# The FFNs' down products by Strassen's scheme: seven block products in place of eight per stretch of FFN units

## The reference

```python
def conv_ffn(xn, w_up, conv_w, conv_b, w_down):
    u = xn @ w_up                                  # 512 x 1024 by 1024 x 5632
    up = jnp.pad(u, ((0, 0), (CONV_WIDTH - 1, 0), (0, 0)))
    c = conv_b
    for j in range(CONV_WIDTH):                    # 3 taps along the tokens
        c = c + conv_w[j] * up[:, j:j + s]
    val, gate = jnp.split(c, 2, axis=-1)
    return (jax.nn.silu(gate) * val) @ w_down      # 512 x 2816 by 2816 x 1024

for layer in range(2):
    h = h + merge_heads(heads) @ w_out[layer]
    h = h + conv_ffn(rmsnorm(h, norm_ffn[layer]), w_up[layer], conv_w[layer], conv_b[layer], w_down[layer])
return rmsnorm(h, norm_final)
```

## Time and profile before

| what | value |
|---|---|
| median of 3 runs | 1738.47 us (1738.30 to 1738.47) |
| span of the profiled execution | 1736.7 us |
| its time by the runs, with what lies around the span | 1738.3 to 1738.47 us, some 1.7 us over the span |
| PE busy | 1724.0 us, 99% of the span |
| POOL busy | 1019.3 us, 59% |
| DVE busy | 947.7 us, 55% |
| ACT busy | 540.9 us, 31% |
| PE's share of the chain that ended last | 96% |

### The profile page before, as it was taken

The page is one execution under the profiler, slowest core; times in us unless marked ns, Lnnn a source line. Parts: engine busy times, 40 slices in busy tenths (PEclk is TensorE's granted clock), DMA queues, the critical chain, the costliest instruction groups (busy, mean ns, idle before and its releaser), DMA issues.

```text
span 1736.7 us, 24721 instructions
## 1 busy us (share of the span) xinstructions
PE 1724.0 (99%) x9676; PEld 1403.0 (81%) x9680; DVE 947.7 (55%) x1893; ACT 540.9 (31%) x1212; POOL 1019.3 (59%) x1046
## 2 busy tenths in 40 slices
PE   9999999999999999999999999999999999999998
PEld 7886787787689877789888888897777988888887
DVE  6997734785643355525661266237775366405643
ACT  4626532213423344432110011036663321101112
POOL 8524556562366744338776677656443587667763
PEclk9999999999999999999999999999999999999999
DMA  6322223221233311114323332323112233243321
GB/s 187 107 80 66 99 77 106 67 92 43 73 122 109 98 49 59 63 49 115 98 92 91 102 96 89 114 73 98 50 55 68 73 109 97 85 117 91 99 93 50
DMA packets 174196, 152.17 MB, mean 88 GB/s; under 512 B 5448, under 2 KB 149192, under 8 KB 174080
## 3 DMA queue, kind: packets, MB, share of 16 engines
q1 hardware_dynamic: 171904, 148.05, 28.1%
q10 hardware_dynamic: 2176, 2.53, 0.4%
HBM read 147.38 MB, written 2.14 MB: 86 GB/s over the span
## 4 chain that ended last, share of the span: by engine, by line
PE 96%; DVE 2%; ACT 1%; issue 0%; DVEq 0%; ACTq 0%
PE ps L302 80%; PE ps L2236 2%; PE ps L2256 2%; PE ps L2271 2%; PE ps L1703 1%; PE ps L373 1%; PE ps L1681 1%; PE ps L2244 1%; PE ps L1618 1%; PE ps L806 1%; PE ps L1639 1%; PE ps L1693 0%; PE ps L1627 0%; PE ps L813 0%; PE ps L756 0%; PE ps L781 0%
## 5 line engine op out<-in xcount | busy, mean ns | idle before, releaser
L146 POOL TENSOR_SCALAR w_hi<-w_raw 128x512 fp32r<-128x512 f32 x512 | 312.2, 637 | 671.9 <-PE ps L302 671.9
L150 POOL TENSOR_TENSOR w_lo<-w_raw,w_hi 128x512 fp32r<-128x512 f32 x512 | 687.2, 1373 | 11.1
L302 PE MATMUL ps<-x_hi,w_hi 128*128 128x512 f32 (+2 forms) x1432 | 532.3, 372 | 0.5 <-DVE x_lo L574 0.4
L302 PE MATMUL ps<-x_hi,w_lo 128*128 128x512 f32 (+2 forms) x1432 | 522.5, 365 | 0.0
L302 PE MATMUL ps<-x_lo,w_hi 128*128 128x512 f32 (+2 forms) x1432 | 522.0, 365 | 0.0
L302 PEld LDWEIGHTS ps<-x_hi,w_hi 128*128 128x128 f32 (+1 forms) x1432 | 269.3, 188 | 60.1 <-issue 16.5
L302 PEld LDWEIGHTS ps<-x_hi,w_lo 128*128 128x128 f32 (+1 forms) x1432 | 269.3, 188 | 44.3
L302 PEld LDWEIGHTS ps<-x_lo,w_hi 128*128 128x128 f32 (+1 forms) x1432 | 269.6, 188 | 40.1
L2553 DVE SCALAR_TENSOR_TENSOR ffn_cv<-ps,col,ffn_cv 128x510 f32<-128x510 f32 (+1 forms) x176 | 131.8, 749 | 192.7 <-ACT ffn_cv L2531 188.1
L2531 ACT ACTIVATE ffn_cv<-ps,col 128x512 f32<-128x512 f32 x88 | 63.8, 776 | 496.6 <-PE ps L302 496.6
L330 DVE TENSOR_TENSOR h<-h,ps 128x512 f32<-128x512 f32 x64 | 43.8, 687 | 258.9 <-PE ps L302 258.9
(11 more groups left out here) (372 smaller groups left out, 2426.5 us busy)
## 6 DMA issues: line engine op xcount, KB each, us to landing
w_raw<-w_up SPq DMA_DIRECT2D x88, 512.0 KB, 5.1
w_raw<-w_down SPq DMA_DIRECT2D x16, 1024.0 KB, 5.0
w_raw<-od_w_in SPq DMA_DIRECT2D x12, 1024.0 KB, 5.2
w_raw<-w_in_fox SPq DMA_DIRECT2D x10, 1024.0 KB, 5.3
w_raw<-w_in_dil SPq DMA_DIRECT2D x10, 1024.0 KB, 5.4
w_raw<-w_out SPq DMA_DIRECT2D x8, 1024.0 KB, 5.0
w_raw<-ev_w_in SPq DMA_DIRECT2D x6, 1024.0 KB, 5.7
w_raw<-w_down SPq DMA_DIRECT2D x8, 768.0 KB, 4.4
```

The source lines that it names most:

```text
L146: ins = pool.tensor_scalar(hi[:, c:min(c + PIECE, size)], raw[:, c:min(c + PIECE, size)], 1.0, 1.0, ALU.mult, ALU.mult)
L150: ins = pool.tensor_tensor(lo[:, c:min(c + PIECE, size)], raw[:, c:min(c + PIECE, size)], hi[:, c:min(c + PIECE, size)].bitcast(F32), ALU. ...
L302: mm = pe.matmul(o, l, r, start=start and i == 0, stop=stop and i == 2)
```

## The change

The down product of a stretch is taken as a 2 x 2 block product: the tokens in two halves of 256, the units in even and odd ones, the output columns in two halves of 512. In place of eight block products it makes seven (Strassen's scheme in Winograd's form), from sums and differences of the blocks.

- The stretches are 8, 8 and 6 units (`PARTS`), so four, four and three k tiles (`kk`) per block product. A block product is 2 token tiles x kk x 3 matmuls of 512 columns, and its weights are one slot. Per stretch the order is 1, 5, 2, 6, 7, 3, 4; products 5 and 2 first leave out the last k tile ("most") and make it up later ("last").
- Weights: POOL splits the slots of products 1, 5 and 2 as before, and makes four combinations of kk pieces of 512 (TENSOR_TENSOR). The `hi` of the slots 6, 7, 3 and 4 is made by ACT, the `lo` by DVE. A third raw buffer of four pieces holds quarter 22; the combinations lie in `w_chain`.
- Activations: a pair of units gives seven operand blocks of 256 tokens. DVE makes four sums of 256 (s1 to s4), ACT the `hi` (one of 256 and three of 512), DVE the `lo` (one of 256 and three of 512). DVE no longer works a unit ahead: conv(u), gate(u), first low, conv(u + 1), gate(u + 1), sums, lows.
- Sums: DVE adds or subtracts PSUM banks into `h` 16 times per stretch (`take`), in order with the weights' lows (`early`). TensorE accumulates on over several products in the same banks, so products 6, 7 and 3 wait for such reads.
- In the seam and the final stage each `last_tile` is now the half of product 3 or 4 for one token tile, 9 matmuls. `Final` takes for each tile the column half that is ready early first.
- The causal mask's place in SBUF serves as a part of the third raw buffer and the mask is loaded again after the first FFN; the tables of the second mixer are loaded after it too. Several semaphores are shared. Elsewhere only the counting of slots changes (`W.nth`).

The core of the diff:

```diff
+class Group:
+    ORDER = ("1", "5", "2", "6", "7", "3", "4")
+    LATE = ("6", "7", "3", "4")
+    def gpsimd(self, pool):
+        W, kk = self.W, self.kk
+        pool.wait_ge(W.loaded[self.a], self.arrived["11"])
+        W.halve(pool, self.slot("1"), W.raw[:, self.a, 0:kk * 512])
+        pool.wait_ge(W.loaded[self.b], self.arrived["12"])
+        if self.lows:
+            pool.wait_ge(W.lo_by_dve, self.lows)
+        for k in range(kk):
+            pool.tensor_tensor(self.chain(k), self.quarter(self.b, k), self.quarter(self.a, k), ALU.subtract).then_inc(W.combined, 1)
+        pool.wait_ge(W.combined, self.sums + kk)
+        W.halve(pool, self.slot("5"), W.chain[:, 0:kk * 512])
+        pool.wait_ge(W.loaded[self.a], self.arrived["21"])
+        W.halve(pool, self.slot("2"), W.raw[:, self.a, 0:kk * 512])
+        pool.wait_ge(W.loaded[RAW], self.arrived["22"])
+        pool.wait_ge(W.split_done, W.nth(self.slot("5")))
+        for k in range(kk):
+            pool.tensor_tensor(self.chain(k), self.quarter(RAW, k), self.chain(k), ALU.subtract).then_inc(W.combined, 1)
+        for k in range(kk):
+            pool.tensor_tensor(self.quarter(self.b, k), self.quarter(RAW, k), self.quarter(self.b, k), ALU.subtract).then_inc(W.combined, 1)
+        pool.wait_ge(W.lo_by_dve, self.lows + 1)
+        for k in range(kk):
+            pool.wait_ge(W.combined, self.sums + kk + k + 1)
+            pool.tensor_tensor(self.chain(k), self.chain(k), self.quarter(self.a, k), ALU.subtract).then_inc(W.combined, 1)
+    def high(self, act, m):      # kk ACTIVATEs of 512, after W.used and W.combined
...
+    def low(self, dve, m):       # kk TENSOR_TENSORs of 512, each after its high
...
-        HALF = FC // 2
+        PARTS = ((0, 8), (8, 8), (16, 6))
...
+            def last_half(self, pe):         # class Down
+                g, kk = self.group, self.group.kk
+                every, most, last = range(kk), range(kk - 1), range(kk - 1, kk)
+                pe.wait_ge(W.split_done, W.nth(g.slot("1")))
+                pe.wait_ge(self.freed.s, self.freed.at(self.u0 + self.n - 3))
+                pe.wait_ge(self.first_ready.s, self.first_ready.at(self.j0 + kk))
+                for t in range(2):
+                    self.sums(pe, "1", "X", t, every, True)
...
+                pe.wait_ge(self.pair_ready.s, self.pair_ready.at(self.j0 + kk - 1))
+                for t in range(2):
+                    self.sums(pe, "5", "Y", t, most, True)
...
+                for t in range(2):
+                    self.sums(pe, "2", "Z", t, most, True)
+                pe.wait_ge(self.pair_ready.s, self.pair_ready.at(self.j0 + kk))
+                for t in range(2):
+                    self.sums(pe, "5", "Y", t, last, False)
+                for t in range(2):
+                    self.sums(pe, "2", "Z", t, last, False)
+                pe.wait_ge(W.lo_by_dve, g.lows + 1)
+                for t in range(2):
+                    pe.wait_ge(self.read.s, self.read.at(1 + t))
+                    self.sums(pe, "6", "X", t, every, False)
+                pe.wait_ge(W.lo_by_dve, g.lows + 2)
+                for t in range(2):
+                    pe.wait_ge(self.read.s, self.read.at(7 + t))
+                    self.sums(pe, "7", "X", t, every, False)
...
+            def early(self, dve):
+                self.take(dve, "X1", 0, "1")
+                self.take(dve, "X1", 1, "1")
+                g.low(dve, "6")
+                self.take(dve, "Y5", 0, "5")
+                self.take(dve, "Y5", 1, "5")
+                self.take(dve, "Z", 0, "2")
+                self.take(dve, "Z", 1, "2")
+                g.low(dve, "7")
+                self.take(dve, "X6", 0, "6")
+                g.low(dve, "3")
+                self.take(dve, "X6", 1, "6")
+                g.low(dve, "4")
+                for t in range(2):
+                    self.take(dve, "X7", t, "7")
+                    self.take(dve, "X7b", t, "7")
...
+                    for u in range(u0, u0 + n, 2):          # DVE, per pair of units
+                        conv(u)
+                        gate(u)
+                        low(u, 1, 0, 1, a11).then_inc(self.first_ready.s, 1)
+                        conv(u + 1)
+                        gate(u + 1)
+                        link(dve.tensor_tensor(s1, a21, a22, ALU.add))
+                        dve.tensor_tensor(s2, s1, a11, ALU.subtract).then_inc(self.made.s, 1)
+                        dve.tensor_tensor(s3, a11, a21, ALU.subtract)
+                        dve.wait_ge(self.made.s, self.made.at(u + 1))
+                        dve.tensor_tensor(s4, a12, s2, ALU.subtract).then_inc(self.made.s, 1)
+                        low(u, 2, 1, 2, cv[:, (u + 1) % 4, 0, :])
+                        low(u, 3, 3, 2, cv[:, u % 4, 1, :])
+                        low(u, 4, 5, 2, cv[:, (u + 1) % 4, 1, :]).then_inc(self.pair_ready.s, 1)
```

More of the change, by code:

```diff
@@ L118, in split @@
[L118 to L146, removed]
@@ new lines, in __init__, with nth, fetch @@
+        self.arrived = [0] * (RAW + 1)
+        self.free = [[] for _ in range(RAW + 1)]
+        self.turn = 0
+        self.by_pool = []
+        self.groups = {}
+        self.combinations, self.acts, self.dves = 0, 0, 0
+    def nth(self, slot):
+        return sum(self.by_pool[:slot + 1])
+    def fetch(self, slot, buffer, kk, nn, pieces):
+        self.arrived[buffer] += 16 * (len(pieces) if buffer < RAW else kk)
+        self.raws.append((slot, buffer, kk, nn, pieces, self.free[buffer]))
+        return self.arrived[buffer]
@@ L154, in parts, with split @@
+    def split(self, pool, until):
+        n = self.cut
+        while n < min(len(self.slots), until + SPLIT):
+            if n in self.groups:
+                self.groups[n].gpsimd(pool)
+                n += 7
+                continue
+            kk, nn, r, need = self.slots[n]
+            pool.wait_ge(self.loaded[r], need)
+            self.halve(pool, n, self.raw[:, r, 0:kk * nn])
+            n += 1
+        self.cut = n
     def parts(self, n):
-        kk, nn, _ = self.slots[n]
+        kk, nn, _, _ = self.slots[n]
@@ L1958, in block_kernel @@
         normed = at("normed", 48, [P, 2, D])
+        W.chain = at("w_chain", 72, [P, SLOT])
+        W.third = [at("w_third0", 80, [P, 512])[:, :]] + [at_a(f"w_third{i}", 2 * i, [P, 512])[:, :] for i in (1, 2)] + [causal[:, :]]
         class Memory:
@@ L2559, in conv, with gate @@
                     dve.sem_inc(self.conv_done.s, 1)
-                def join(u):
-                    _, i = self.units[u]
+                def gate(u):
                     dve.wait_ge(self.silu_done.s, self.silu_done.at(u + 1))
-                    if u == HALF:
-                        dve.wait_ge(W.used, self.out[0].slots[1][-1] + 1)
+                    part, i = self.units[u]
+                    if i == 0 and part > 0:
+                        dve.wait_ge(W.used, w_down[self.layer, part - 1].slot("4") + 1)
@@ L2578, in vector @@
                         for tile in range(T):
-                            self.out[part].add(dve, half, tile)
+                            d.add(dve, 1, tile)
         class Final:
```

443 lines of the change are left out of this document (302 added, 141 removed).

## The result

Four runs of the kernel after gave 1779.64 to 1780.13 us, median 1779.97, against 1738.38 (1737.71 to 1738.47) for the kernel before beside them: ratio 1.0239, 95% interval 1.0225 to 1.0254. The forecast was 1783 us, with its own range 1768 to 1790.

What follows compares the result with a forecast made beforehand. TensorE, busy 99% of the span, was taken as the bound: 1738.5 - 29.9 (matmuls) + 49.6 (stretches of four) + 20.8 (of three) + 3.7 (seam and end) = 1782.7 us. Own range 1768 to 1790; 8 in 10, 1722 to 1800.

Steps and rivals of the forecast that it cites:

- The bound and the saving: TensorE, busy 99% of the span, bounds the kernel; 132 fewer down-product matmuls at 0.2267 us take off 29.9 us.
- DVE's price beside POOL: DVE operations on SBUF alone wait for POOL's running piece: 1.8 us per low of 512, 1.5 per sum of 256.
- Rival A: POOL's pieces fall beside DVE's convs, so DVE pays its prices alone: 1720.7 us, chance 0.17.
- 1, product 1: Stretches with four k tiles: the last even unit's first operand is there at +2.4, needed at 0; wait 2.4 us.
- Step 2: Stretches of four: last pair ready at +19.3, TensorE through products 1, 5 (most), 2 (most) at +16.0; wait 3.3 us.
- step 3: Stretches of four, product 6: DVE's four lows, behind the pair and two additions, take 6.3 against 2.7 us; wait 3.5.
- 4, product 7: Stretches of four: DVE's additions and lows take 8.2 against 5.4 us, wait 2.7; the second half waits 0.5.
- The stretches of three: Two six-unit stretches, same chains with less cover: waits 7.3, 0.4, 2.2 and 0.5, 10.4 us each, 20.8 in both.
- Seam and end: Seam: wait 1.8 us for tile 1's row; end: the last tile queues behind three on ACT, 1.9 us; sum 3.7.
- Rival C: TensorE is granted 1.2 GHz after its waits of 7 us in the stretches of three: 1790 or 1797 us, chance 0.10.
- Rival B: POOL is done a few us earlier, its pauses fall where DVE is late, half the difference: 1751.7 us, chance 0.22.
- three signs against the forecast: Profile after: DVE's operations there show 0.7 us, PE's waits sum to under 30 us, or TensorE waits for POOL's splits.

Runs made afterwards that it cites:

- e1: The changed kernel with all of POOL's FFN pieces, splits and combinations, cut from 512 columns to 8: 1717.45 us, ratio 0.988.
- e3: The changed kernel with each POOL combination piece replaced by three linked memsets of 512 columns, which write SBUF and read nothing: 1731.79 us, ratio 0.9962.
- e6: The changed kernel with useless matmuls put where TensorE waits, in front of products 5 (last), 6 and 7: 1775.08 us, ratio 1.021.
- e8: The changed kernel with DVE's two loops of the final stage made one, each tile's early half just before its late half: 1778.03 us, ratio 1.0227.
- e7: The changed kernel with DVE's lows of the weights of products 6, 7 and 4 as one instruction each: 1774.06 us, ratio 1.0204.
- e5: The changed kernel with POOL's pieces 256 columns wide in place of 512, nothing left out: 1788.44 us, ratio 1.0288.

## Why the prediction was right

Sizes are distances between matmul starts, against the pace of 0.2267 us.

**The bound and the saving: right.** 308 matmuls per group; 132 fewer at 0.2267, 29.9 us. e1 shows 21 of them once POOL is out of the way.

**DVE's price beside POOL: right.** The forecast took 1.5 us for a sum of 256, a value that no row had; the medians of the four sums over all 22 pairs are 1.40, 1.40, 1.49 and 0.83, and beside a POOL in TENSOR_TENSORs all four take 1.40 to 1.51. 1.8 for a low was right too, in the last pair: three took 5.15, where two of them were forecast behind POOL (4.1). In the pair before it two of the three lows take 1.09, beside POOL's shorter TENSOR_SCALARs. Rival A needed prices alone. Its condition was made in e1, and came to 1717.45 against the 1720.7 worked out for it.

**Why a port and not POOL's time.** e3 holds POOL's occupation and takes away its reads, and the lows fall to 0.69 to 0.72. The Trainium skill (SBUF — State Buffer, "Who interferes with whom") says that a DVE instruction with two SBUF inputs contends with a GpSimd one that reads SBUF, not with one that only writes it. Both halves agree with this case: a sum takes 1.40 us beside TENSOR_TENSORs, 0.42 beside memsets.

**The stretches of four: mechanism and sum right, the parts mixed.** The four steps gave 12.4 us. Measured is 11.65: 1.9 in front of product 1, and 9.8 within the down product. Around the first one, PE's rows (duration, [idle before, which is less than the lost time, since a modelled end lies 0.16 us or more behind the next possible start]):

```profile
875.85 0.47 PE L428 MATMUL ps<-w_hi,ffn_a_hi 128*128 128x512 f32 x1 [1.73 <-DVE ffn_a_lo L2838]
...
891.95 0.50 PE L428 MATMUL ps<-w_hi,ffn_a_hi 128*128 128x512 f32 x1 [2.22 <-DVE ffn_a_lo L2838]
...
893.79 0.63 PE L428 MATMUL ps<-w_hi,ffn_a_hi 128*128 128x512 f32 x1
...
897.77 0.50 PE L428 MATMUL ps<-w_hi,ffn_a_hi 128*128 128x512 f32 x1 [1.22 <-DVE w_lo L281]
...
905.64 0.47 PE L428 MATMUL ps<-w_hi,ffn_a_hi 128*128 128x512 f32 x1 [2.15 <-DVE h L2684]
```

| step, in front of | forecast | measured |
|---|---|---|
| 1, product 1 | 2.4 | 1.9 |
| 2, product 5 (last) | 3.3 | 2.4 |
| 3, product 6 | 3.5 | 1.6 |
| 4, product 7 | 2.7 and 0.5 | 2.3 |
| slow matmuls, two spells | none | 2.9 |

The remaining 0.5 us is in small waits. Step 2 was forecast 0.9 too long since the last odd unit's base doesn't wait for the first low: ACT starts it at 874.66, right behind the high and 0.7 us after the last up product, where the forecast had 2.3:

```profile
874.66 1.43 ACT L2777 ACTIVATE ffn_cv<-ps,col 128x512 f32<-128x512 f32 x2
```

From there the pair takes 17.2 us (to 891.90), forecast 17.0. Steps 3 and 4 were forecast too long as well, step 3 by half, partly because the slow matmuls (0.63 us in the row) fill the time in front of product 6; with the clock at 1.00 (e6) that wait is 1.7 in the profile in place of 1.2. The sum came out near because TensorE is held to DVE's pace there: whether it stands still or runs slowly matters little.

**The stretches of three: right.** Forecast 10.4, measured 9.7 and 9.5: the wait of 7.3 is 6.7, and some eight slow matmuls (1.8) stand where small waits were counted.

**Seam and end.** Forecast 1.8 at the seam, measured 1.6. The end is the term that was too small: 1.9 forecast, 4.2 measured (10.6 us from the last down matmul, 6.4 before). The interval of 2.66 us between ACT's tiles was right, but the forecast let the first one start on time. The DVE rows at the end:

```profile
1759.26 2.47 DVE L2684 TENSOR_TENSOR h<-h,ps 128x512 f32<-128x512 f32 x4
1761.65 0.68 DVE L2922 TENSOR_TENSOR res<-h,final_gain 128x512 f32<-128x512 f32 x1
...
1763.64 0.68 DVE L2922 TENSOR_TENSOR res<-h,final_gain 128x512 f32<-128x512 f32 x1
...
1764.31 0.67 DVE L2684 TENSOR_TENSOR h<-h,ps 128x512 f32<-128x512 f32 x1
```

The final stage's four early halves (1761.65 to 1764.31) stand on DVE ahead of tile 0's sum. It is ready to be read then, but starts 2.7 us late. e8 shows that moving the four doesn't win the time back.

**The sum.** 4 x 11.65 + 9.7 + 9.5 + 1.6 + 4.2 = 71.6; less 29.9, 41.7. The spans differ by 41.6.

**What of it is luck.** That the measured time lies 3 us from the forecast. With the clock at 1.00 (e6) a stretch of four loses 10.4 us, so its waits alone were forecast 2.0 too long, 8 us in all. Two things that the forecast left out or made too small, the clock (5 us) and the end (2.3), nearly cancel that. Without the clock's share the time would be e6's 1775, still in the range: the mechanism doesn't need the luck, the distance of 3 us does.

**Rival C happened beside the forecast, not in place of it.** The clock fell to 0.93 and 0.87 in the rows of the last section. The matmuls themselves run 0.43 us apart, 1.2 GHz, behind waits of 2.4 us, where C had counted only those of 7 surely. Its price of 7 to 14 us was too high and in the wrong place: e6 gives 5, all in the stretches of four, and nothing in those of three, for which the 7 were worked out. The Trainium skill (TensorE: Matmul & The Clock Gate, "What's actually happening") says that an idle TensorE falls to half its clock; the trace agrees. By that rule C was likely and I gave it 0.10; had I taken it in whole, the sum of 1790 to 1797 would have been further off than the forecast.

**Rival B, half the loss: did not happen.** POOL runs from 878.02 to 895.97 without a pause, through all of step 2. Its one pause then falls into step 3:

```profile
897.80 5.95 POOL L259 TENSOR_TENSOR w_chain<-w_chain,w_raw 128x512 f32<-128x512 f32 x4 [1.83 <-DVE w_lo L281]
```

The last two of the four lows there take 0.68 us each, the first two 1.81 and 1.77. That is what the forecast's own step 3 had (1.8, 1.8, 0.7, 0.7), so it brings nothing of B's gain.

**What was to show it.** Waits for DVE in front of 1, 5 (last), 6 and 7 came at 1.2 to 2.2 us in the profile, and 6.6 in the stretches of six units; "2 to 4" was too much for products 1 and 6. The median of 1.5 to 1.8 us for DVE's sums and lows in the second half of the up products was not met: it is 1.40 for the sums and 1.09 for the lows of 512, and only the last pair shows 1.40 to 1.51 and 1.75 to 1.78. PE busy is 62 us under the span, not 85: slow matmuls count as busy. None of the three signs against the forecast appeared.

**What stays open.** Lateness of the combinations is worth 13 us in e3, with memsets a little longer than the real pieces; how much of that would show with pieces of the true length was not run. The exchange between waits and slow matmuls was read in the stretches of four; in those of three only its sum is known.

## What to carry to other kernels

When work moves from the bounding engine to DVE and POOL, cost each DVE operation on SBUF alone at its price beside a reading POOL, and count how many of them stand between the last input and the next matmul: here eight per pair (a gate, four sums, three lows), in a place with 9.5 to 13.6 us of cover. Fewer, longer DVE operations lose fewer turns (e7), and smaller POOL pieces help only while POOL has time to spare (e5). A control in which the other engine's operations are kept in number and cut to 8 columns finds such a cost in one run; that it is the reads, and not work that comes late, took a second one (e3).

## What the runs showed of the hardware that was not expected

- A POOL memset of 512 columns takes 527 ns, and DVE's operations beside it run nearly at their price alone (721 and 687 ns for lows that took 1125 and 881; 684 in e1).
- TensorE dropped to 1.2 GHz for about seven matmuls (0.43 us apart) after it had stood still for only 2.4 us, and not at once: the first four matmuls behind the wait still start 0.23 to 0.34 us apart (891.95 to 892.99), then the slow ones come. The longest wait before was 1.5 us, with no such trace.
- In alternation both sides pay: POOL's combination piece takes 1.44 us beside sums of 256 columns (883.65) and 1.74 beside lows of 512; in e7, beside operations of 2048, one takes 3.44 (893.09).
